# One core: a second token block's down product, key columns 0 to 79, by row gathers in the stage before the dense product; the dense groups there cut to 256 tokens and kept in PSUM

## The reference, cut to what matters

```python
def block(args):
    tb, eb, gb = args
    u = jnp.take(expert_u, eb, axis=0)
    act = jax.nn.gelu(jnp.einsum('ted,td->te', u, tb)) * gb
    vv = jnp.take(expert_v, eb, axis=0)
    return jnp.einsum('te,ted->td', act, vv)
```

## Time and profile before

| | us |
|---|---|
| three runs | 4038.86, 4040.24 (median), 4046.48 |
| span of the profiled execution | 4036.8 |
| PE busy in it | 3976.2 |
| stage of 44 plain up units in it | 2459 to 2938 |
| down stage in it | 2938 to 4013 |

### The profile page before, as it was taken

The page is one execution under the profiler, slowest core; times in us unless marked ns, Lnnn a source line. Parts: engine busy times, 40 slices in busy tenths (PEclk is TensorE's granted clock), DMA queues, the critical chain, the costliest instruction groups (busy, mean ns, idle before and its releaser), DMA issues.

```text
span 4036.8 us, 53696 instructions
## 1 busy us (share of the span) xinstructions
PE 3976.2 (98%) x19085; PEld 3435.1 (85%) x19085; DVE 2474.3 (61%) x3519; ACT 1227.3 (30%) x1299; POOL 926.3 (23%) x670
## 2 busy tenths in 40 slices
PE   8999999999999999999999999999999999999998
PEld 5887777787888788888888888888899999999997
DVE  7565777469534654545767673222257878888885
ACT  4333322334223322222333332222222222222223
POOL 1100000322111345453000000000033444444432
PEclk9999999999999999999999999999999999999999
DMA  4543333653543454546777678666768888888883
GB/s 168 195 148 130 121 118 118 211 185 102 186 146 136 162 184 159 185 159 211 244 237 244 237 250 304 216 217 217 233 232 308 311 315 305 323 304 326 299 323 131
DMA packets 240049, 867.73 MB, mean 215 GB/s; under 512 B 22600, under 2 KB 61016, under 8 KB 172272
## 3 DMA queue, kind: packets, MB, share of 16 engines
q1 hardware_dynamic: 96720, 454.07, 30.7%
q10 hardware_dynamic: 94080, 204.49, 16.3%
q0 software_dynamic: 49184, 208.36, 14.9%
HBM read 768.25 MB, written 232.81 MB: 248 GB/s over the span
## 4 chain that ended last, share of the span: by engine, by line
PE 62%; DVE 7%; DMA 5%; issue 3%; ACT 2%; POOL 1%; DVEq 0%; SPq 0%; ACTq 0%; POOLq 0%
PE mm L1973 15%; PE mm L1974 15%; PE mm L1975 15%; DMA raw<-stream 4%; PE pv L1973 2%; PE pv L1974 2%; PE pv L1975 2%; DVE wlo L1129 2%; PE sc L1973 1%; PE sc L1975 1%; PE sc L1974 1%; ACT whi L686 1%; DVE acc L1895 1%; POOL el L638 1%; PE st L1975 1%
## 5 line engine op out<-in xcount | busy, mean ns | idle before, releaser
L1129 DVE TENSOR_TENSOR wlo<-raw,whi 128x2048 fp32r<-128x2048 f32 x329 | 756.0, 2298 | 760.0 <-ACT whi L686 759.0
L686 ACT ACTIVATE whi<-raw 128x2048 fp32r<-128x2048 f32 x378 | 723.8, 1915 | 494.6 <-issue 194.5
L1973 PE MATMUL mm<-t_hi,whi 128*128 128x512 f32 x2048 | 799.0, 390 | 4.5 <-DVE t_lo L1695 3.1
L1974 PE MATMUL mm<-t_lo,whi 128*128 128x512 f32 x2048 | 797.4, 389 | 0.0
L1975 PE MATMUL mm<-t_hi,wlo 128*128 128x512 f32 x2048 | 796.8, 389 | 0.0
L1973 PEld LDWEIGHTS mm<-t_hi,whi 128*128 128x128 f32 x2048 | 384.6, 188 | 86.2 <-DVE t_lo L1695 6.4
L1975 PEld LDWEIGHTS mm<-t_hi,wlo 128*128 128x128 f32 x2048 | 384.5, 188 | 80.5
L1974 PEld LDWEIGHTS mm<-t_lo,whi 128*128 128x128 f32 x2048 | 384.7, 188 | 77.3
L1973 PE MATMUL mm<-hn_hi,whi 128*128 128x512 f32 x960 | 378.0, 394 | 4.4 <-DVE wlo L1129 4.4
L1974 PE MATMUL mm<-hn_lo,whi 128*128 128x512 f32 x960 | 374.7, 390 | 0.0
L1975 PE MATMUL mm<-hn_hi,wlo 128*128 128x512 f32 x960 | 374.3, 390 | 0.0
(11 more groups left out here) (450 smaller groups left out, 7190.4 us busy)
## 6 DMA issues: line engine op xcount, KB each, us to landing
raw<-stream SPq DMA_DIRECT2D x380, 1024.0 KB, 4.9
ev_d<-stream ACTq DMA_DIRECT2D x128, 1024.0 KB, 6.1
up_d<-sgl ACTq DMA_DIRECT2D x128, 256.0 KB, 2.1
g_d<-gst ACTq DMA_DIRECT2D x12, 2048.0 KB, 11.5
gg<-g_d SPq DMA_DIRECT2D x15, 1536.0 KB, 11.8
gl<-up_d SPq DMA_DIRECT2D x120, 192.0 KB
spill<-stage ACTq DMA_DIRECT2D x44, 256.0 KB, 2.0
xm_d<-xms POOLq DMA_DIRECT2D x12, 512.0 KB, 5.5
```

The source lines that it names most:

```text
L686: act.activation(whi[:, k, :], raw[:, k, :], ACT.Copy).then_inc(hi_done, 1)
L1129: dve.tensor_tensor(wlo[:, k, :], raw[:, k, :], whi[:, k, :].bitcast(F32), ALU.subtract)\
L1973: pe.matmul(out, lh, rh, start=start, stop=False)
L1974: pe.matmul(out, lh, rl, start=False, stop=False)
```

## The change

Key columns j of 0 to 79 (groups 0 to 9) of the third token block (tokens 256 to 383) are now also done by row gathers, in the plain stage. There DVE weighs three slots behind each `wlo` (`early_slots`; two in the last four units) into `acc1`, from three buffers `gv1` filled by `rows1`, with the values `el1` gathered in batches of 12 (`activations1`). Rows with j of 80 and more are skipped by a bounds check and their weights are zero. `stored_up` stores the third block's activations once more to `up1_d` for the first 84 units. The `gv1` buffers lie where `h2` lies, so its 4 MB reload moves from the end of the hot stage to behind the last early slot; `acc1` lies where `gst` lies, so DVE and POOL wait for the last store of `g_d` first. The dense groups 0 to 9 run with 256 columns and sum into 16 half banks of PSUM through all ten groups (`first_down`); DVE adds those once, in group 9 (`add_first`). Groups 10 to 15 stay at 384 columns. The fourth block's slots are spread anew: 7 in each of groups 1 to 9, 12 in each of 10 to 14, 5 in the last, in batches of the same sizes. The 44 row copies of the plain stage are issued in four earlier stages. ACT's and DVE's loops over the groups are written out.

```diff
+TE = TD - P
+G1 = 10
+G2 = GROUPS_D - G1
+J1 = 8 * G1
+FIRST_COPIES = N_PLAIN // 4
+BATCH1 = 12
+
+SLOTS1 = _counts(SLOTS, (3, N_UP - N_PLAIN - 8 + 4), (2, 4))
+BATCHES1 = _counts(SLOTS, (BATCH1, SLOTS // BATCH1), (SLOTS % BATCH1, 1))
+SLOTS2 = _counts(SLOTS, (7, G1 - 1), (12, G2 - 1), (5, 1))
...
                     sp.wait_ge(actlo_done, 8 * g + v + 7)
-                    sp.wait_ge(up_out[v % 2], 64 * g + 16 * (v // 2) + 80)
-                    sp.dma_start(gl[:, v % 2, :], up_d[8 * g + 8 + v, :, 0:TD]).then_inc(upn_in[v % 2], 16)
+                    sp.wait_ge(up_out[v % 2], _up_count(4 * g + v // 2 + 5))
+                    nt_ = TD if g + 1 >= G1 else TE
+                    sp.dma_start(gl[:, v % 2, 0:nt_], up_d[8 * g + 8 + v, :, 0:nt_]).then_inc(upn_in[v % 2], 16)
...
+            def activations1(b):
+                s0, size = BATCHES1[b]
+                for s in range(s0, s0 + size):
+                    pool.indirect_dma_start(el1[:, s:s + 1], None, ups1_flat,
+                                            bass.IndirectOffsetOnAxis(ap=idx_e1[:, s:s + 1], axis=0)).then_inc(el_in, 16)
+
+            def rows1(s):
+                if s >= 3:
+                    pool.wait_ge(acc_done, s - 2)
+                pool.indirect_dma_start(gv1[s % 3][:], None, ev_d,
+                                        bass.IndirectOffsetOnAxis(ap=idx_v1[:, s:s + 1], axis=0),
+                                        bounds_check=J1 * P - 1, oob_is_err=False).then_inc(gv_in[s % 3], 16)
+
+            pool.wait_ge(small_done, 2)
+            for k in range(2):
+                pool.wait_ge(up_out[k], _up_count(J1 // 2))
+            activations1(0)
             pool.wait_ge(hot_used, 8 + 16 * BLOCKS)
-            pool.dma_start(h2[:], h2_d).then_inc(h2_copied, 16)
             for b in range(2):
                 pool.wait_ge(gst_out[b], 16 * (BLOCKS // 2))
+            pool.wait_ge(ev_out, 16 * N_UP)
+            for s in range(3):
+                rows1(s)
+            pool.dma_start(gg[:, 0, 0:TE // 32, :], gg_src[0][:, 0:TE // 32, :]).then_inc(g_in, 16)
+            next_batch = {s0 + 3: b + 1 for b, (s0, _) in enumerate(BATCHES1[:-1])}
+            next_load = {SLOTS1[N_UP - N_PLAIN - 9 + v][0] + 3: v for v in range(8)}
+            for s in range(3, SLOTS):
+                if s in next_batch:
+                    pool.wait_ge(ac_done, next_batch[s])
+                    activations1(next_batch[s])
+                if s in next_load:
+                    v = next_load[s]
+                    if v >= 2:
+                        pool.wait_ge(actlo_done, v - 1)
+                    load_up(v, v % 2)
+                rows1(s)
+            pool.wait_ge(acc_done, SLOTS)
+            pool.dma_start(h2[:], h2_d).then_inc(h2_copied, 16)
...
+            next_batch = {s0 + 3: b + 1 for b, (s0, _) in enumerate(SLOTS2[:-1])}
             for s in range(3, SLOTS):
-                if s % BATCH == 3:
-                    pool.wait_ge(ac_done, s // BATCH + 1)
-                    activations(s // BATCH + 1)
+                if s in next_batch:
+                    pool.wait_ge(ac_done, len(BATCHES1) + next_batch[s])
+                    activations(next_batch[s])
                 rows(s)
...
+                    gather_rows(FIRST_COPIES + c, k)
...
+                    gather_rows(FIRST_COPIES + SC + q, k)
...
+                for i in (2 * h, 2 * h + 1):
+                    gather_rows(*((GROUPS_E - 1, i - 4) if i >= 4 else (GROUPS_E - 3 + i // 2, i % 2)))
...
+                    gather_rows(FIRST_COPIES + SC - 2 + p, 2 + k)
...
+                if not plain:
+                    act.dma_start(up1_d[n], sgl[:, k, TE:TD]).then_inc(up_out[k], 16)
...
-                    stored_up(m - (U_FILL - N_FILL) // 2, k)
-                    gather_rows(N_PLAIN // 4 + r, s)
+                    stored_up(m - (U_FILL - N_FILL) // 2, k, plain=True)
...
+            def early_slots(i):
+
+                for s in range(SLOTS1[i][0], SLOTS1[i][0] + SLOTS1[i][1]):
+                    for b, (s0, _) in enumerate(BATCHES1):
+                        if s == s0:
+                            weights1(b)
+                    weigh(s, True)
...
+            def down_group(g):
+                s0, size = SLOTS2[g - 1] if g else (0, 0)
                 for v in range(8):
...
+                    if g == G1 and v == 3:
+                        add_gathered(0, TE)
+                        dve.wait_ge(acct_free, 4)
+                    if v % 2 == 1 and g == G1 - 1:
+                        add_first(v // 2)
+                    if v % 2 == 1 and g >= G1:
                         add_down(g, v // 2)
-                    if slots:
-                        for c in (range(2) if v == 0 else range(v + 1, v + 2)):
-                            weigh(BATCH * (g - 1) + c, c % 3, 3 * (g - 1) + c // 3 + 1, peeled and c == 0)
-
-            with dve.Fori(U_PLAIN // 2, U_DOWN // 2 - 4) as m:
-                for k in range(2):
-                    next_lo(m, k)
+                    if v == 0 and size:
+                        weights(g - 1)
+                    for s in range(s0 + size * v // 8, s0 + size * (v + 1) // 8):
+                        weigh(s, False)
...
+            for b in range(2):
+                dve.wait_ge(gst_out[b], 16 * (BLOCKS // 2))
+            for i in range(N_UP - N_PLAIN - 8):
+                next_lo(U_PLAIN // 2 + i // 2, i % 2)
+                early_slots(i)
...
+                early_slots(N_UP - N_PLAIN - 8 + v)
             dve.wait_ge(h2_copied, 32)
...
+            def first_down(g, v, first=False, final=False):
+
+                q, h, k = v // 2, v % 2, v % 2
+                pe.wait_ge(lo_done, U_DOWN + 8 * g + v + 1)
+                if v < 2:
+                    pe.wait_ge(actlo_done, 8 * g + 4 * v + 4)
+                for b in range(4):
+
+                    if first and h == 0 and b % 2 == 0:
+                        pe.matmul((vo2[0] + vo2[1])[2 * q + b // 2][:].rearrange("p (r c) -> p r c", r=4), zero_r[:],
+                                  zero_r[:].unsqueeze(1).to_broadcast([P, 4, P]), start=True, stop=False)
+                    for jj in range(4):
+                        last = mm3(halves1[4 * q + b], *w(k, 512 * jj + P * b), acts[:, (g + 1) % 2, 0, 4 * h + jj, :],
+                                   acts[:, (g + 1) % 2, 1, 4 * h + jj, :], False,
+                                   final and h == 1 and jj == 3 and b % 2 == 1)
+                last.then_inc(half_done, 1)
+
...
+            def gathered(n, sums):
+
+                pe.wait_ge(acc_done, SLOTS * (n + 1))
+                for b in range(4):
+                    pe.wait_ge(v_free, 8 + 16 * n * (G2 - 1) + b + 1)
+                    for d in range(4):
+                        last = pe.transpose(vo2[0][b][:, P * d:P * d + P],
+                                            sums[:, P * (4 * b + d):P * (4 * b + d) + P], ident[:])
+                    last.then_inc(acct_done, 1)
+
```

More of the change, by code:

```diff
@@ L53, with _counts, _up_count @@
 FIN_V = 11
-BATCH = 9
+TE = TD - P
[4 more added lines that the diff above has]
+BATCH1 = 12
+def _counts(total, *parts):
+    starts, at = [], 0
+    for size, times in parts:
+        for _ in range(times):
+            starts.append((at, min(size, total - at)))
+            at += starts[-1][1]
+    assert at == total, at
+    return starts
+SLOTS1 = _counts(SLOTS, (3, N_UP - N_PLAIN - 8 + 4), (2, 4))
+BATCHES1 = _counts(SLOTS, (BATCH1, SLOTS // BATCH1), (SLOTS % BATCH1, 1))
+def _up_count(pairs):
+    return 16 * pairs + 16 * min(pairs, N_PLAIN // 2)
+SLOTS2 = _counts(SLOTS, (7, G1 - 1), (12, G2 - 1), (5, 1))
 O_GLU, O_QKV, O_YB, O_WO, O_UP = 60, 92, 132, 148, 164
@@ new lines, in _, with weigh @@
+            FILLS1 = [(SLOTS + 2 - b) // 3 for b in range(3)]
+            def weigh(s, early):
+                buf, sum_, col_, base, fills = (gv1, acc1, ac1, 0, 0) if early else (gv, acc, ac, SLOTS, FILLS1[s % 3])
+                dve.wait_ge(gv_in[s % 3], 16 * (fills + s // 3 + 1))
+                if s == 0:
+                    dve.tensor_scalar(sum_[:], buf[0][:], col_[:, 0:1], None, ALU.mult).then_inc(acc_done, 1)
+                else:
+                    dve.wait_ge(acc_done, base + s)
+                    dve.scalar_tensor_tensor(sum_[:], buf[s % 3][:], col_[:, s:s + 1], sum_[:], ALU.mult, ALU.add)\
@@ L1911, in down_group @@
+            def down_group(g):
+                s0, size = SLOTS2[g - 1] if g else (0, 0)
                 for v in range(8):
                     down_lo(g, v)
-                    if v == 0 and not slots:
+                    if v == 0:
                         dve.wait_ge(gn_in, 16 * g + 16)
                     dve.wait_ge(upn_in[v % 2], 64 * g + 16 * (v // 2) + 16)
-                    gate((g + 1) % 2, v, 8 * g + 8 + v)
-                    act_low(g % 2, v, 8 * g + 8 + v)
-                    if v % 2 == 1:
-                        add_down(g, v // 2)
@@ new lines, in _ @@
+            for v in range(8):
```

(31 more changed lines are left out.)

206 lines of the change are left out of this document (113 added, 93 removed).

## The result

The changed kernel took 4212.97 us (median of 4 runs, 4204.09 to 4216.86) against 4041.79 us for the kernel before beside it: ratio 1.0421, 95% interval 1.0408 to 1.0433, slower. The forecast was 4091 us. The profiled execution has a span of 4213.5 us, 176.7 more than before's.

What follows compares the result with a forecast made beforehand. PE was taken to bound the kernel before. Terms -113 + 88 + 19 + 2 + 46 + 5 + 2 + 2 = +51 took the span from 4036.8 to 4088, the median to 4091 us; own case 4060 to 4125 (48%).

Steps and rivals of the forecast that it cites:

- Plain stage: Up units with the early row gathers: 51.2 us per twelve slots and four units, 567 us against 479, +88.
- Later landings just hide: Plain stage, rows after a period's fourth: issued 6.7 us ahead against a 6.2 us landing, so no wait within 27.0 us.
- The bounds of 49 and 57.2: Plain stage: low and high time in us for a period of twelve slots, around 51.2; +68 and +142 in all.
- Dense groups: Groups 0 to 9 at 256 columns: 5.9 us a unit in group 0, 7.0 after, -113 in all.
- The ring of `raw`: Dense groups: two load buffers set the pace, 14.0 us for two units with a landing of 7.8.
- loads land as if alone: Rival, 20%: loads in groups 1 to 9 land near 5 us, 86 us less there, 4005 in all, faster.
- Joint: Between up and down stages: DVE waits for the 17.1 us reload of h2, 27 us in all, +19.
- Groups 10 to 14: Late groups: DVE's chain has no slack, so a 10.4 us wait behind twelve value gathers gives 77.7 a group, +46.
- Last group: Final group: five weighs instead of two, with the last two rows landing late, +5.
- Copies: The 44 row copies moved to earlier stages: +2, range 0 to +12, since loads of heads may wait.
- Clock: PE's clock coming back after the stop at the joint: 2 us taken, between nothing and 5.8.
- A slower early chain: Rival, 20%: plain stage at 57.2 us a period, 4145 in all, with gathers slower beside DVE's work.

Runs made afterwards that it cites:

- e7: Changed kernel with the last block's late slots as before: 9 in each of groups 1 to 14, 2 in group 15; 4202.1 us.
- e1: Changed kernel with four row buffers instead of three for the early slots; 4145.0 us.
- e5: Changed kernel with four row buffers and early value gathers in batches of 4 instead of 12; 4083.1 us.
- e2: Changed kernel with early value gathers in batches of 3 instead of 12, still three row buffers; 4134.0 us.
- e3: Changed kernel without early slots 3 to 127 of the third block (output lacks them), h2 reloaded at the plain stage's start; 4010.1 us.
- e11: Changed kernel with late slots 9, 9 and 2, values gathered 5 before a group's fourth row and 4 before its eighth; 4178.6 us.
- e9: Changed kernel with many edits joined (including four row buffers, 28 values early), weights two slots after issue, late values in batches of 3; 4126.0 us.

## Why the prediction was right or wrong, step by step

The sign was right, the size not: +51 forecast, +177 in the profile.

- **Plain stage, +88 forecast, +197.1: 109 of the 126 us by which the sum is off.** The start was 15.6 us (16 forecast), and all behind the ninth period 93.3 (90). The nine periods between took 566.9, forecast 461. The step that failed is "Later landings just hide: a slot's row is issued once the slot three before is weighed, so two weighs and a split, 6.7 us, ahead". It left out what stands before a landing's end: the gather itself takes POOL 1.9 to 2.9 us beside DVE's work, two of them can stand one behind the other, and a row lands 7.3 us in the middle and up to 10.8 after its gather's start (in e7's trace), not 6.2. The 6.7 us do not cover that; three buffers turn in 12.5 to 13.5 us, not in DVE's 9. e1 and e5 show it: with a fourth buffer 68.7 us go. The bounds of 49 and 57.2 let the batch and one landing vary, never these 27.0, which took 37.1 in the period shown, and the mean of 62.8 lies outside. The part up to the fourth weigh took 27.2 us for 24.2, by the batch alone: it begins 1.2 us behind the weights, since POOL is still at a row, and takes 20.4, not 18, while the row behind it is there after 5.5, not 6.2. e2 shows it as a cause of its own.
- **Dense groups, -113, measured -111.2.** Group 0 took 6.1 us a unit over its last seven (5.9 forecast), groups 1 to 9 took 507.4 / 72 = 7.05 (7.0). The ring of `raw` held: DVE waited for `whi` and ACT for `raw` there (96.1 and 107.2 us), and DVE for no row but one (1.7 us). The rival in which loads land as if alone did not hold: landings in the middle were 7.2 us in e3 and 7.4 in e7 over such groups (7.8 forecast), 4.9 at least in e3. The Trainium skill's page "DMA: Bandwidth & Descriptors", section on the anatomy of one DMA, gives 4.4 us for 1 MB by its fit, which it states for DMAs issued by GpSimd, while these loads are issued by SP; here the measured 7.2 and 7.4 decide.
- **Joint, +19, measured +16.0**: 20.0 us from the last gelu to the start of the second split, against 24.6 in the forecast (its 27 holds the split itself), since the reload landed 13.1 us after its issue, not 17.1.
- **Groups 10 to 14, +46 and 2 for transposes, measured +53.1**: five waits with 45.4 us, for four of 10.4. (The forecast's 77.7 a group is 77.4 by its own terms, 67.0 + 10.4, so its +46 should read +44.)
- **Last group, +5, measured +11.1**, undersized: with two slots there instead of five, in e7 and e11, it took 98.6, as before.
- **Copies, +2, measured +10.1 to the first gelu.** The range of 0 to 12 held; what the forecast named as a possible wait were the loads of heads, and it was the landing of a store that was waited for.
- **Clock.** Forecast 2, for the joint alone. There the granted clock is 0.50 from 3168, when PE starts again, to 3173, and 0.98 from 3173 to 3178, so half speed for 5 us, some 2.5 us lost (an estimate). In the plain stage its mean is 0.88 and it falls behind the long stops (0.50 from 2644 to 2656, 0.96 from 2656 to 2679); there DVE and POOL, not PE, set the end.
- **Rivals and signs.** "A slower early chain" (20%) pointed at the right stage, and with the right row: a gather of 1.90 us beside DVE. Its 57.2 us a period and 4145 still were too little, and above 4170 less than 10% was left. The sign "gathers with a bounds check that take POOL longer than 2 us" came: 0.99 to 3.12 us, 1.89 in the middle.

## What to carry to other kernels

For a ring of buffers, add up the whole turn (what stands ahead in the issuing queue, the issue itself at its loaded pace, the landing in the middle, the use) and divide by the buffers; if that is over the consumer's pace, each turn costs the difference, however well one landing seems to hide. Count a queue in instructions: a burst ahead of a load is a delay of the load, and a semaphore wait ahead of it is another. An edit that removes one wait of an engine may only move it: in e9 the waits for values went, and waits for rows came.
